# Up projections of a two-block network: the weight sums of rounds 1 to 21 made on GpSimd instead of VectorE

## The chip, the cores and the metric

The kernel runs on one core of a Trainium2 chip, as one program with five instruction streams: TensorE (PE in the profile; its weight loads are PEld), VectorE (DVE), ScalarE (ACT), GpSimd (POOL) and SyncE (SP), which issues the large weight transfers. The engines meet only through semaphores. The metric is the device time of one execution in microseconds (us), the median of several runs; lower is better. All data is fp32.

## The reference, cut to what matters

The program computes two blocks after each other on a sequence of 512 tokens with 1024 features. The first has two layers, each a mixer and a gated feed-forward network with a causal convolution of three taps:

```
def _conv_ffn(h, w_up, conv_w, conv_b, w_down):        # h: 512 x 1024, D_FF = 2816
    u, v = jnp.split(h @ w_up, 2, axis=-1)
    uc = conv_b + sum(shifted(u, j) * conv_w[j] for j in range(3))
    return (jax.nn.silu(uc) * v) @ w_down

for l in range(2):
    mod = silu(c) @ ada_w[l] + ada_b[l]                # six modulation vectors
    ...
    h = x * (1.0 + sc2) + sh2
    y = _conv_ffn(h, ffn_w_up[l], ffn_conv_w[l], ffn_conv_b[l], ffn_w_down[l])
    x = _layer_norm(ALPHA * x + g2 * y, ln_g[l, 1], ln_b[l, 1])
```

The second block (a recurrent and Fourier mixer, then a retention layer) follows and is not touched. What matters here is `h @ w_up`, twice, and the product `c @ ada_w`, which is spread over other stages in small tiles.

## The kernel before, in words

**The up projection.** `w_up` of a layer comes in 22 slabs of 1 MB, each with 128 columns of u and 128 of v. One slab is one round (`n` from 0 to 21). TensorE computes a round by Strassen's scheme in Winograd's form: the slab is a 2 by 2 grid of blocks (u or v, even or odd row blocks), the activations H another (even or odd row blocks, first or second half of the tokens). Seven block products take the place of eight; each is 4 matmuls of 128x128 weights by 256 columns, and each matmul stands in the profile as two instructions, so a round is 56 of them. The price is sums of blocks. Four "left sums" are needed for each slab, four tensor_tensor operations of 128x512 elements (lines 660 to 663). Round `n` writes them to buffer `LS[n % 2]`. The "right sums" of H are made once a layer.

**The order on TensorE** (`ffn_pe`). Each round from 1 on: wait for the slab; two products that need no left sums (16 instructions); wait for "left sums" `n`; two products with sums; two more; a last one. At its end the slab's slot is free. There are two slots, so SyncE issues slab `n + 2` when round `n` ends.

**The order on VectorE** (`ffn_dve`). In each round it first makes the left sums of round `n + 1`, then adds the products out of PSUM (lines 770 to 779: 256 columns each, one operand in SBUF and one in PSUM), applies two taps (781, 782), works on modulation tiles (350, or 354 and 357), and multiplies by the gate (788). The taps, the modulation work and line 788 have two operands in SBUF. ScalarE copies the first product, applies one tap and the SiLU.

**Modulation tiles.** `ada_w` comes as tiles of 128x1024 (512 KB), issued by GpSimd (line 377) into three buffers `late[j % 3]`. The issue of tile `j` waits for VectorE to be done with tile `j - 3`. VectorE uses two tiles a round in layer 0 (one operation each), one tile a round in layer 1 (two operations).

**GpSimd** (`ffn_pool`). In the up projection of a layer it issues tiles up to those for round 10, makes the four right sums of the first down projection (`first_right_pool`, 128x1024 elements each, from the results of rounds 0 to 7), issues tiles up to those for round 19, and then makes, for each of 12 steps of the down projection, that step's left sums, with tiles issued between them.

The two buffers of the left sums lie elsewhere: `LS[1]` takes the place of R, which ScalarE reads until it has written the last block of XA (line 629). So the sums of round 1 wait for the event ("norm", l, 0) "x" 7.

Of the kernel before, what the change touches and what calls it, by code (L numbers as in the profile page):

```python
# [9 lines left out]
ALU = mybir.AluOpType  # L10
# [5 lines left out]
DT = D // P  # L16
# [5 lines left out]
FT = FF // P  # L22
# [124 lines left out]
PE, DVE, ACTE, POOL = "pe_done", "dve_done", "act_done", "pool_done"  # L147
# [7 lines left out]
class Core:  # L155
# [53 lines left out]
    def p(self, name, a=0, n=None):  # L209
        at, size = P_AT[name]  # L210
        return self.par[:, at + a:at + a + (size - a if n is None else n)]
# [39 lines left out]
def settled(k, ins, *event):  # L251

    ins.then_inc(*k.says(DVE, *event))
    k.nc.vector.wait_ge(*k.now(DVE))
# [59 lines left out]
def dense_dve(k, name, n_tiles, splits, evac, first=0, deep=None):  # L314
# [3 lines left out]
    for n in range(n_tiles):  # L318
# [6 lines left out]
ADA_UP = [[range(N_ADA[0] + 2 * n, N_ADA[0] + 2 * n + 2) for n in range(FT)],  # L325
          [range(N_ADA[0] + 61 + n, N_ADA[0] + 62 + n) for n in range(FT)]]
# [15 lines left out]
def ada_tile_dve(k, j):  # L342

    v = k.nc.vector
    v.wait_ge(*k.when("ada in", j))
    part, tile = ada_home(j)
    w = k.early[:, j % EARLY, :] if j < N_EARLY else k.late[:, j % LATE, :]
    bias = k.p(("ada_b0", "ada_b1", "ada_b2_0", "ada_b2_1")[part], tile, 1)
    if part < 2:
        v.tensor_tensor_reduce(w, w, k.c_row[:], 1.0, bias, ALU.mult, ALU.add, k.MOD[part][:, tile, :])\  # L350
            .then_inc(*k.says(DVE, "ada used", j))
    else:
        v.wait_ge(*k.when("ada used", j - 1))
        v.tensor_tensor_reduce(k.junk[:], w, k.c2_rows[:, 0, :], 1.0, bias, ALU.mult, ALU.add, k.MOD2[part - 2][:, tile, 0:1])\
            .then_inc(*k.says(DVE))
        v.wait_ge(*k.now(DVE))
        v.tensor_tensor_reduce(w, w, k.c2_rows[:, 1, :], 1.0, bias, ALU.mult, ALU.add, k.MOD2[part - 2][:, tile, 1:2])\  # L357
            .then_inc(*k.says(DVE, "ada used", j))
# [12 lines left out]
def late_tiles_pool(k, first, last):  # L371

    g = k.nc.gpsimd
    for j in range(first, last):
        if j >= N_EARLY + LATE:
            g.wait_ge(*k.when("ada used", j - LATE))
        g.dma_start(k.late[:, j % LATE, :], k.dram["ada_rest"][j]).then_inc(*k.lands(f"late_in{j % LATE}", "ada in", j))  # L377


def ffn_pool(k, l, first):  # L380

    def issued(until):
        nonlocal first
        last = min(until + LATE, N_ADA[0] + 96)
        late_tiles_pool(k, first, max(first, last))
        first = max(first, last)
    issued(ADA_UP[l][10].stop)
    first_right_pool(k, l)
    issued(ADA_UP[l][FT - 3].stop)
    for it in range(ND):  # L390
        down_left_pool(k, l, it)
        issued(ADA_UP[l][FT - 1].stop if it == 0 else ADA_DOWN[l][it - 1].stop)
    issued(ADA_DOWN[l][-1].stop)
# [239 lines left out]
def left_blocks(k, l, n):  # L633

    wv = k.slab_view(f"w_up{l}", n, DT, 2 * P).rearrange("p (i e) (m n) -> p i e m n", e=2, m=2)
    return {(m, e): wv[:, :, e, m, :] for m in range(2) for e in range(2)}


def right_block(k, e, s, i0=0, i1=4):
    return k.H[:, 2 * i0 + e:2 * i1:2, s * HALF:(s + 1) * HALF]  # L640
# [6 lines left out]
def product(k, n, j):  # L647
    bank, s = PRODUCT_AT[j]
    return k.ps[:, 4 * (n % 2) + bank, s * HALF:(s + 1) * HALF]


def left_sums_dve(k, l, n):

    v, A, S = k.nc.vector, left_blocks(k, l, n), k.LS[n % 2]
    v.wait_ge(*k.when("slab", k.slab(f"w_up{l}", n)))
    if n >= 2:
        v.wait_ge(*k.when("products", l, n - 2, 3))
    elif n == 1:
        v.wait_ge(*k.when(("norm", l, 0), "x", DT - 1))
    v.tensor_tensor(S[:, 2, :, :], A[0, 0], A[1, 0], ALU.subtract).then_inc(*k.says(DVE))  # L660
    settled(k, v.tensor_tensor(S[:, 0, :, :], A[1, 0], A[1, 1], ALU.add))
    settled(k, v.tensor_tensor(S[:, 1, :, :], S[:, 0, :, :], A[0, 0], ALU.subtract))
    v.tensor_tensor(S[:, 3, :, :], A[0, 1], S[:, 1, :, :], ALU.subtract).then_inc(*k.says(DVE, "left sums", l, n))  # L663


def right_sums_dve(k, l, h):

    v, R = k.nc.vector, k.RS4
    v.wait_ge(*k.when(("norm", l, 0), "h", 4 * h + 3))
    B = {(e, s): right_block(k, e, s, 2 * h, 2 * h + 2) for e in range(2) for s in range(2)}  # L670
    t1, t2, t3, t4 = (R[:, j, 2 * h:2 * h + 2, :] for j in range(4))
    v.tensor_tensor(t3, B[1, 1], B[0, 1], ALU.subtract).then_inc(*k.says(DVE))
    settled(k, v.tensor_tensor(t1, B[0, 1], B[0, 0], ALU.subtract))
    settled(k, v.tensor_tensor(t2, B[1, 1], t1, ALU.subtract))
    v.tensor_tensor(t4, B[1, 0], t2, ALU.subtract).then_inc(*k.says(DVE, "right sums", l, h))
# [80 lines left out]
def ffn_dve(k, l):  # L756

    v = k.nc.vector
    v.memset(k.U[:, :, 0:2], 0.0).then_inc(*k.says(DVE, "ffn pad", l))
    for h in range(2):  # L760
        right_sums_dve(k, l, h)
    for n in range(FT):
        U, C, X, V = k.U[:, n % 2, :], k.C[:, n % 2, :], k.PX, k.PV
        p = lambda j: product(k, n, j)
        w = lambda j: k.p(f"conv{l}", 4 * n + j, 1)
        if n + 1 < FT:
            left_sums_dve(k, l, n + 1)
        first = k.P1[:, n % 2, :]
        v.wait_ge(*k.when("first product", l, n))
        v.tensor_tensor(U[:, 2:HALF + 2], first, p(2), ALU.add).then_inc(*k.says(DVE))  # L770
        v.wait_ge(*k.when("products", l, n, 1))
        settled(k, v.tensor_tensor(X[:, 0, :], first, p(6), ALU.add))
        settled(k, v.tensor_tensor(X[:, 1, :], X[:, 0, :], p(5), ALU.add))
        v.wait_ge(*k.when("products", l, n, 2))
        v.tensor_tensor(U[:, HALF + 2:T + 2], X[:, 1, :], p(3), ALU.add).then_inc(*k.says(DVE, "ffn u", l, n))  # L775
        settled(k, v.tensor_tensor(X[:, 2, :], X[:, 0, :], p(7), ALU.add))
        v.wait_ge(*k.when("products", l, n, 3))
        v.tensor_tensor(V[:, 0:HALF], X[:, 2, :], p(4), ALU.add).then_inc(*k.says(DVE))
        v.tensor_tensor(V[:, HALF:T], X[:, 2, :], p(5), ALU.add).then_inc(*k.says(DVE, "ffn v", l, n))
        v.wait_ge(*k.when("ffn tap", l, n))  # L780
        settled(k, v.scalar_tensor_tensor(C, U[:, 1:T + 1], w(1), C, ALU.mult, ALU.add))
        v.scalar_tensor_tensor(C, U[:, 0:T], w(0), C, ALU.mult, ALU.add).then_inc(*k.says(DVE, "ffn conv", l, n))
        if l == 0 and n == 0:
            v.wait_ge(*k.when("c2"))
        for j in ADA_UP[l][n]:
            ada_tile_dve(k, j)
        v.wait_ge(*k.when("ffn silu", l, n))
        v.tensor_tensor(k.G[:, n, :], C, V[:], ALU.mult).then_inc(*k.says(DVE, "ffn g", l, n))
# [27 lines left out]
def down_left_pool(k, l, it):  # L816

    g, (h, q) = k.nc.gpsimd, DOWN[it]
    A, S = down_left(k, l, it)
    g.wait_ge(*k.when("slab", k.slab(f"w_down{l}_{h}", q)))  # L820
    if it:
        g.wait_ge(*(k.when("down products", l, it - 2, 3) if it >= 2 else k.when("products", l, FT - 1, 3)))
    g.tensor_tensor(S[1], A[1, 0], A[1, 1], ALU.add).then_inc(*k.says(POOL))
    g.wait_ge(*k.now(POOL))
    g.tensor_tensor(S[2], S[1], A[0, 0], ALU.subtract).then_inc(*k.says(POOL))
    g.tensor_tensor(S[3], A[0, 0], A[1, 0], ALU.subtract).then_inc(*k.says(POOL))
    g.wait_ge(*k.now(POOL))
    g.tensor_tensor(S[4], A[0, 1], S[2], ALU.subtract).then_inc(*k.says(POOL, "down left", l, it))


def first_right_pool(k, l):

    g = k.nc.gpsimd
    B, R = down_right(k, 0)
    g.wait_ge(*k.when("ffn g", l, 7))
    g.tensor_tensor(R[1], B[0, 1], B[0, 0], ALU.subtract).then_inc(*k.says(POOL))
    g.wait_ge(*k.now(POOL))
    g.tensor_tensor(R[2], B[1, 1], R[1], ALU.subtract).then_inc(*k.says(POOL))
    g.tensor_tensor(R[3], B[1, 1], B[0, 1], ALU.subtract).then_inc(*k.says(POOL))
    g.wait_ge(*k.now(POOL))  # L840
    g.tensor_tensor(R[4], B[1, 0], R[2], ALU.subtract).then_inc(*k.says(POOL, "down right", l, 0))
# [3173 lines left out]
```

## Time and profile before

| | us |
|---|---|
| median of 3 runs (2493.9 to 2502.34) | 2498.15 |
| profiled execution, device time | 2495.48 |
| span of that execution's trace | 2494.1 |
| busy in the span: PE / DVE / ACT / POOL | 2334.1 / 1659.2 / 640.2 / 235.9 |

The span runs from the first to the last instruction; some 1.4 us of the device time lie around it. The up projection of layer 0 runs from about 360 to 631 us of the span, that of layer 1 from about 828 to 1100 us. The chain of work that ended last is TensorE for 84% and VectorE for 11%; the up projections' matmuls (line 683) alone are 20% of it. A wait of another engine costs time only if TensorE comes to wait in its turn.

In the rows below, "left_sums<-ring" means: writes the tile left_sums, reads the slab's slot. A bracket at the end of a line is the time that the engine sat idle before it, and what ended that.

### The profile page before, as it was taken

To read this page: it belongs to the slowest core of one execution; us is meant where nothing else is said; L and a number is where in the kernel's file an instruction comes from. 1 tells how busy PE (TensorE), PEld (TensorE's weight loads), DVE (VectorE), ACT (ScalarE), POOL (GpSimd) and SP (SyncE) were. 2 spreads that over 40 slices of the span, in tenths; PEclk is the share of its full clock that TensorE was granted. 3 is DMA by queue.
4 is the path that set the end of the run, shared out by engine and by line. 5 is a ranking of instruction groups with operands and counts; after the bars stand their busy time and mean duration, and the time that the engine had idled before them with its cause. 6 is when DMAs were issued, how large, how long until landed. Compare 5 with 4: busy or idle time off the path is not lost.

```text
span 2494.1 us, 39647 instructions
## 1 busy us (share of the span) xinstructions
PE 2334.1 (94%) x17066; PEld 1693.8 (68%) x17066; DVE 1659.2 (67%) x2800; ACT 640.2 (26%) x1314; POOL 235.9 (9%) x261
## 2 busy tenths in 40 slices
PE   7988889999997999999999999999997999999997
PEld 3675548888884688888756676676675654546973
DVE  3784378798799888879847879779787123232442
ACT  1323331111002311111043354444444212101111
POOL 2000000020541002024400000000000000000000
PEclk9999999999999999999999999999998999999999
DMA  8232135555432233343221101001010212111102
GB/s 329 90 113 76 60 134 169 172 170 181 161 131 89 85 128 126 135 139 132 95 98 70 40 19 35 21 20 37 3 36 19 85 51 84 51 52 66 35 18 101
DMA packets 42224, 227.99 MB, mean 91 GB/s; under 512 B 4737, under 2 KB 4865, under 8 KB 25793
## 3 DMA queue, kind: packets, MB, share of 16 engines
q1 hardware_dynamic: 21456, 140.56, 15.7%
q0 software_dynamic: 20016, 82.79, 9.8%
q8 instruction: 135, 2.21, 0.4%
q10 hardware_dynamic: 576, 2.11, 0.3%
q14 instruction: 41, 0.33, 0.0%
HBM read 219.14 MB, written 6.29 MB: 90 GB/s over the span
## 4 chain that ended last, share of the span: by engine, by line
PE 84%; DVE 11%; ACT 2%; issue 2%; DMA 1%; POOL 0%; SPq 0%; DVEq 0%; ACTq 0%; POOLq 0%
PE ps L683 20%; PE ps L2283 10%; PE ps L905 8%; PE ps L307 7%; PE ps L3383 3%; PE ps L2064 3%; PE ps L1039 3%; PE ps L455 2%; PE ps L1715 2%; PE ps L3572 2%; PE ps L2293 2%; PE ps L2302 2%; PE ps L3003 1%; PE ps L2971 1%; PE ps L2990 1%
## 5 line engine op out<-in xcount | busy, mean ns | idle before, releaser
L2283 PE MATMUL ps<-H,ring 128*128 128x256 f32 (+1 forms) x832 | 271.4, 487 | 5.4 <-ACT LW L2502 2.6
L683 PE MATMUL ps<-right_sums,left_sums 128*128 128x256 f32 x1056 | 242.8, 379 | 2.7 <-DVE left_sums L663 2.7
L2283 PEld LDWEIGHTS ps<-H,ring 128*128 128x128 f32 x832 | 157.4, 190 | 112.9 <-issue 92.8
L683 PEld LDWEIGHTS ps<-right_sums,left_sums 128*128 128x128 f32 x1056 | 200.5, 190 | 30.6 <-DVE left_sums L663 3.5
L307 PE MATMUL ps<-H,ring 128*128 128x512 f32 (+1 forms) x480 | 181.5, 535 | 0.9 <-DVE ls_tmp L3250 0.9
L683 PE MATMUL ps<-H,ring 128*128 128x256 f32 x704 | 164.2, 385 | 12.7 <-ACT H L626 12.7
L905 PE MATMUL ps<-G,ring 128*128 128x256 f32 x704 | 159.8, 379 | 0.0
L683 PEld LDWEIGHTS ps<-H,ring 128*128 128x128 f32 x704 | 134.6, 192 | 35.6 <-issue 12.8
L307 PEld LDWEIGHTS ps<-H,ring 128*128 128x128 f32 x480 | 91.1, 190 | 88.3 <-issue 84.9
L905 PEld LDWEIGHTS ps<-G,ring 128*128 128x128 f32 x704 | 133.8, 190 | 18.2
L377 POOL DMA_DIRECT2D ada_late<-ada_rest x104 | 56.2, 540 | 684.7 <-DVE mod L357 373.5
L750 ACT ACTIVATE C<-U,params_sb 128x512 f32<-128x512 f32 x44 | 35.9, 816 | 314.9 <-DVE U L775 314.9
L683 PE MATMUL ps<-H,left_sums 128*128 128x256 f32 x352 | 86.9, 388 | 0.0
L3383 PE MATMUL ps<-ring,H 128*128 128x256 f32 x384 | 85.9, 379 | 0.0
L2064 PE MATMUL ps<-O,ring 128*128 128x512 f32 (+1 forms) x256 | 83.6, 486 | 0.6 <-DVE H L2007 0.6
L683 PE MATMUL ps<-right_sums,ring 128*128 128x256 f32 x352 | 83.5, 379 | 0.0
L2007 DVE TENSOR_SCALAR H<-ps,scalars 128x512 f32<-128x512 f32 (+1 forms) x24 | 15.3, 661 | 97.7 <-ACT sq_ctx L2024 61.2
L3383 PEld LDWEIGHTS ps<-ring,H 128*128 128x128 f32 x384 | 72.0, 190 | 12.1 <-issue 3.1
L683 PEld LDWEIGHTS ps<-H,left_sums 128*128 128x128 f32 x352 | 68.2, 194 | 10.8 <-ACT H L626 1.4
L350 DVE CUSTOM_DVE_ANT_0 ada_late<-ada_late,c_row,params_sb 128x1024 f32<-128x1024 f32 x56 | 69.9, 1280 | 6.3 <-DMA ada_late<-ada_rest 6.2
L683 PEld LDWEIGHTS ps<-right_sums,ring 128*128 128x128 f32 x352 | 66.9, 190 | 9.1
L2064 PEld LDWEIGHTS ps<-O,ring 128*128 128x128 f32 x256 | 48.5, 190 | 34.0 <-issue 30.6
(593 smaller groups left out, 4704.2 us busy)
## 6 DMA issues: line engine op xcount, KB each, us to landing
ada_late<-ada_rest POOLq DMA_DIRECT2D x104, 512.0 KB, 3.7
ring<-w_up SPq DMA_DIRECT2D x44, 1024.0 KB, 4.8
ring<-w_down SPq DMA_DIRECT2D x16, 1024.0 KB, 4.9
ring<-od_in SPq DMA_DIRECT2D x16, 1024.0 KB, 4.8
ring<-ev_in SPq DMA_DIRECT2D x15, 1024.0 KB, 4.8
ada_early<-ada_rest POOLq DMA_DIRECT2D x24, 512.0 KB, 4.7
ada_first_sb<-ada_first SPq DMA_DIRECT2D x8, 1024.0 KB, 16.3
ring<-ab_in SPq DMA_DIRECT2D x7, 1024.0 KB, 6.4
```

The lines of the kernel that those rows point to most:

```text
L307: mm = pe.matmul(k.ps[:, (n % deep) * nb + b, 0:tn], wv[:, kk, a * P:(a + 1) * P], rhs[:, kk, t0:t0 + tn], start=(kk == 0), stop=(kk == kt ...
L350: v.tensor_tensor_reduce(w, w, k.c_row[:], 1.0, bias, ALU.mult, ALU.add, k.MOD[part][:, tile, :])\
L377: g.dma_start(k.late[:, j % LATE, :], k.dram["ada_rest"][j]).then_inc(*k.lands(f"late_in{j % LATE}", "ada in", j))
L455: mm = pe.matmul(k.ps[:, n, :], k.W8[:, kk, n * P:(n + 1) * P], k.H[:, kk, 0:T], start=(kk == 0), stop=(kk == DT - 1))
L683: return pe.matmul(product(k, n, j), lhsT[:, i, :], rhs[:, i, :], start=(i == 0), stop=(i == 3))
L905: mm = pe.matmul(product(k, it, j), left[:, i, :], right[:, i, :], start=(i == 0), stop=(i == ni - 1))
L1039: mm = pe.matmul(k.ps[:, bank, :], wv[:, kk, (i % 2) * P:(i % 2 + 1) * P], k.H[:, kk, 0:T], start=(kk == 0), stop=(kk == DT - 1))
L1715: return pe.matmul(out, wv[:, kk, (n % 2) * P:(n % 2 + 1) * P], rhs, start=start, stop=stop)
L2064: mm = k.nc.tensor.matmul(k.ps[:, 2 * (n % 2) + b, 0:tn], wv[:, kk, (n % 2) * P:(n % 2 + 1) * P], k.O[:, kk, t0:t0 + tn], start=(start and ...
L2283: mm = pe.matmul(k.ps[:, bank + b, 0:tn], wv[:, kk, (i % 2) * P:(i % 2 + 1) * P], k.H[:, kk, t0:t0 + tn], start=(kk == 0), stop=(kk == DT ...
L2293: mm = k.nc.tensor.matmul(k.ps[:, bank + n, 0:tn], lhsT, rhs[:, t0:t0 + tn], start=True, stop=True)
L3383: mm = pe.matmul(k.ps[:, 3 + 4 * (u % 2), 0:256], k.H[:, kk, t * P:(t + 1) * P], wv[:, kk, :], start=(kk == 0), stop=(kk == DT - 1))
```

## The change

The left sums of round 0 stay on VectorE (they are made before the stage). Those of rounds 1 to 21 move to GpSimd, with the same four operations in another order, and the tiles' issue is put between them: after the sums of round `n`, the tiles up to those for round `n - 2`, plus three. `first_right_pool` comes after the sums of round 12 and the issue behind them.

```
 def ffn_pool(k, l, first):
...
-    issued(ADA_UP[l][10].stop)
-    first_right_pool(k, l)
+    issued(ADA_UP[l][0].start)
+    for n in range(1, FT):
+        left_sums_pool(k, l, n)
+        if n >= 2:
+            issued(ADA_UP[l][n - 2].stop)
+        if n == 12:
+            first_right_pool(k, l)
     issued(ADA_UP[l][FT - 3].stop)
...
+def left_sums_pool(k, l, n):
+
+    g, A, S = k.nc.gpsimd, left_blocks(k, l, n), k.LS[n % 2]
+    g.wait_ge(*k.when("slab", k.slab(f"w_up{l}", n)))
+    g.wait_ge(*(k.when("products", l, n - 2, 3) if n >= 2 else k.when(("norm", l, 0), "x", DT - 1)))
+    g.tensor_tensor(S[:, 0, :, :], A[1, 0], A[1, 1], ALU.add).then_inc(*k.says(POOL))
+    g.wait_ge(*k.now(POOL))
+    g.tensor_tensor(S[:, 1, :, :], S[:, 0, :, :], A[0, 0], ALU.subtract).then_inc(*k.says(POOL))
+    g.tensor_tensor(S[:, 2, :, :], A[0, 0], A[1, 0], ALU.subtract).then_inc(*k.says(POOL))
+    g.wait_ge(*k.now(POOL))
+    g.tensor_tensor(S[:, 3, :, :], A[0, 1], S[:, 1, :, :], ALU.subtract).then_inc(*k.says(POOL, "left sums", l, n))
...
 def ffn_dve(k, l):
...
-        if n + 1 < FT:
-            left_sums_dve(k, l, n + 1)
         first = k.P1[:, n % 2, :]
```

## Rows read from the trace of the kernel before

**Rows 1.** Busy time per engine and instructions (x) of one stretch: PE, PEld, DVE, ACT, POOL, clock, DMA
```profile
870.00:970.00 100.00, 100.00 (x465) 88.04 (x464) 80.89 (x150) 15.57 (x26) 4.26 (x9) 1.00 0.40 136
```

**Rows 2.** Waits of TensorE over the span: who waited for whom, us, times, longest
```profile
PE ps L902 <- DVE H L984: 5.2, 2, 2.7
...
PE ps L905 <- DVE down_right_last L861: 3.8, 2, 2.7
PE ps L905 <- POOL ring L828: 3.1, 3, 1.4
...
PE ps L683 <- DVE left_sums L663: 2.7, 2, 1.4
```

**Rows 3.** TensorE in order of time, around round 12 of each layer: start, length
```profile
508.89 3.62 PE L683 MATMUL ps<-H,ring 128*128 128x256 f32 x16
513.78 1.56 PE L683 MATMUL ps<-right_sums,left_sums 128*128 128x256 f32 x6 [1.27 <-DVE left_sums L663]
...
964.68 3.62 PE L683 MATMUL ps<-H,ring 128*128 128x256 f32 x16
...
976.77 3.62 PE L683 MATMUL ps<-H,ring 128*128 128x256 f32 x16
981.78 3.72 PE L683 MATMUL ps<-right_sums,left_sums 128*128 128x256 f32 x16 [1.40 <-DVE left_sums L663]
```

**Rows 4.** VectorE in the same time, layer 1
```profile
965.62 0.74 DVE L781 SCALAR_TENSOR_TENSOR C<-U,params_sb,C 128x512 f32<-128x512 f32 x1
...
967.07 1.28 DVE L354 CUSTOM_DVE_ANT_0 junk<-ada_late,c_rows,params_sb 128x1024 f32<-128x1024 f32 x1
...
969.60 0.69 DVE L788 TENSOR_TENSOR G<-C,product_v 128x512 f32<-128x512 f32 x1
970.21 3.25 DVE L660 TENSOR_TENSOR left_sums<-ring 128x512 f32<-128x512 f32 x1
```

**Rows 5.** GpSimd in the same time: the four right sums of the first down projection
```profile
970.53 2.37 POOL L836 TENSOR_TENSOR down_right<-G 128x1024 f32<-128x1024 f32 x1
972.97 2.70 POOL L838 TENSOR_TENSOR down_right<-G,down_right 128x1024 f32<-128x1024 f32 x1
...
978.50 2.67 POOL L841 TENSOR_TENSOR down_right<-G,down_right 128x1024 f32<-128x1024 f32 x1
```

**Rows 6.** One operation of the left sums, all 44: ns min/median/max
```profile
L660 DVE TENSOR_TENSOR left_sums<-ring x44: 682/686/3245, 351.4 to 1080.7; 128x512 f32<-128x512 f32 x44
```

**Rows 7.** GpSimd: tile issues, and first and last of four sums of a down step
```profile
629.69 1.10 POOL L377 DMA_DIRECT2D ada_late<-ada_rest  x2
...
1093.03 1.26 POOL L823 TENSOR_TENSOR down_left<-ring 128x512 f32<-128x512 f32 x1 [12.07 <-DMA ring<-w_down]
...
1096.94 1.27 POOL L828 TENSOR_TENSOR ring<-ring,down_left 128x512 f32<-128x512 f32 x1
```

**Rows 8.** SyncE's slab issues from 964 on, and the time to landing of w_up slabs
```profile
964.88 26.16 SPq L273 DMA_DIRECT2D ring<-w_up  x3
...
DMA to landing us min/median/max: 4.6/4.8/6.0
```

**Rows 9.** DMA issues from 340 to 620 us: modulation tiles, median us to landing
```profile
ada_late<-ada_rest POOLq DMA_DIRECT2D x41, 512.0 KB, 4.2
```

**Rows 10.** GpSimd and VectorE late in the down steps, in order of time
```profile
701.54 0.99 POOL L826 TENSOR_TENSOR ring<-ring 128x384 f32<-128x384 f32 x1
...
1216.77 1.98 POOL L826 TENSOR_TENSOR ring<-ring 128x384 f32<-128x384 f32 x1
...
1215.99 1.90 DVE L354 CUSTOM_DVE_ANT_0 junk<-ada_late,c_rows,params_sb 128x1024 f32<-128x1024 f32 x1
```

**Rows 11.** VectorE and TensorE at round 1 of layer 1, in order of time
```profile
839.53 0.69 DVE L660 TENSOR_TENSOR left_sums<-ring 128x512 f32<-128x512 f32 x1 [1.58 <-ACT XA L629]
...
843.82 3.62 PE L683 MATMUL ps<-H,ring 128*128 128x256 f32 x16
847.27 3.62 PE L683 MATMUL ps<-right_sums,left_sums 128*128 128x256 f32 x16
```

## The prediction

> **What bounds the kernel now.** I read the views in this order: busy time by stretch, TensorE's waits, then the engines in order of time around the places where TensorE waits. The first shows a TensorE that is busy for all of a 100 us stretch of up projection at full granted clock, while VectorE is busy for 80.9 us of it and GpSimd for 4.3 [rows 1]. A round starts every 12.09 us (964.68 to 976.77 [rows 3]). So the 80.9 us are not a bound as such: shortening VectorE's work gains only where TensorE waits for it. Of such waits on the left sums there are two in the whole trace, 2.7 us together [rows 2], one in each layer, in round 12. In other rounds the products with sums start 3.45 us after the round does (843.82 to 847.27 [rows 11]). In round 12 it is 4.89 us in layer 0 and 5.01 us in layer 1 [rows 3], so 1.44 and 1.56 us late, 3.0 us in all. The cause stands beside it: GpSimd makes its four right sums from 970.53 to 981.17, and VectorE's left sums, 0.69 us by their median [rows 6], take 3.25 us there [rows 4, 5]. Everything else that the change touches is hidden behind TensorE.
>
> **What is removed.** 42 sets of left sums with four operations each leave VectorE: 168 x 0.69 us = 116 us, or 2.8 us of each round. All but the two sets at round 12 lie beside TensorE's work, so 113 us of them are worth nothing. What is worth something is the 3.0 us above, and only if nothing else is late at that place.
>
> **What is added in an ordinary round.** I count from the start of TensorE's round n - 1. SyncE issues slab n at +0.2 us, and it lands 4.8 us later, at +5.0 [rows 3, 8]. GpSimd has no left sums of w_up in the trace, but it does the same four operations on the same 128x512 shapes in the down steps: from 1093.03 to 1098.21, 5.2 us [rows 7]. The lower bound is that. VectorE's line 788, with two operands in SBUF, starts about +4.9 (969.60 in the round of 964.68 [rows 3, 4]), so I add 0.4 us for one collision: done at +10.6. The sums are wanted at 12.09 + 3.45 = +15.5. That leaves 4.9 us of cover. Two things could eat it. The tiles are now issued behind the sums, at +10.6 and +11.2 (0.55 us each [rows 7]) in place of right behind VectorE's use, and each takes 4.2 us to land [rows 9]: they are in flight when SyncE issues the next slab at +12.3. Bounds for what that adds to the slab: nothing, or at most a whole tile's 4.2 us, and the sums are then done at +14.8, still in time. And the collisions with VectorE could be four rather than one: next to VectorE's operations of 1.90 us a GpSimd operation takes 1.98 us where the same one takes 0.99 us elsewhere [rows 10], so 1.0 us each and 5.2 + 4.0 = 9.2 us, done at +14.2. Only both together miss. I take 0 us of TensorE's time for each of the 40 ordinary rounds.
>
> What waits behind the sums in GpSimd's queue is the tile issue. In layer 0 a tile issued at +11.2 lands at +15.4, or +3.3 of the next round, where VectorE, relieved of its sums, wants its second tile at about +3.7: no wait, or one of 1 us that ends long before round n + 2 wants the products read out. In layer 1 the tiles are a round ahead. The issue itself waits for a tile used in the round before, long done.
>
> **Round 1.** The sums wait for ScalarE's last XA block and started on VectorE at 839.53. On GpSimd they end at 839.5 + 5.2 = 844.7, and are wanted at 847.27 [rows 7, 11]: 2.6 us of cover in layer 1. Layer 0 has the same pattern with slightly less. Cost 0, at most 1 us.
>
> **Round 13, where it gets tight.** The four right sums (10.64 us, 970.53 to 981.17 [rows 5]) now stand between the left sums of rounds 12 and 13 in one in-order queue. Counted from the start of round 11: sums of round 12 done at +10.6; tiles issued until +11.7 in layer 0 (two) and +11.2 in layer 1 (one); right sums until +22.3 and +21.8; left sums of round 13 until +27.5 and +27.0. They are wanted at 2 x 12.09 + 3.45 = +27.6. So without more collisions this just fits. But VectorE now comes with its taps, its modulation operations and line 788 (0.74, 1.28 and 0.69 us [rows 4]; two taps, two modulation operations, one product) in the middle of GpSimd's chain. The 10.64 us hold some collision already: three operations took 2.67 to 2.80 us where the first took 2.37 [rows 5]. By rows 10 a modulation operation costs GpSimd 0.9 to 1.0 us; two of them 1.8 and line 788 0.4, less 0.7 for the two smaller collisions they replace, gives 1.5 us. Done at +29.0 and +28.5: TensorE waits 1.4 and 0.9 us, 2.3 in all. Bounds: nothing, and all eight operations hit by 1.0 us each, less the 1.0 us in the 10.64: 7.0 us more, +34.5 and +34.0, so waits of 6.9 and 6.4 us, 13.3 in all. I lean to the lower end, since VectorE has five such operations a round and they cannot meet eight. VectorE loses some 6 us there, but the products of round 12 need only be read out before round 14. Rounds 14 on start with GpSimd back in step, 4 us ahead of the need.
>
> **What the Trainium skill says.** The trace has a VectorE operation of 0.69 us stretched to 3.25 us beside one of GpSimd of 2.4 us [rows 4 to 6]. The Trainium skill (SBUF — State Buffer, "Who interferes with whom") makes that a lock on a shared read interface: an operation with two SBUF inputs on VectorE and a reading one on GpSimd exclude each other for whole instructions. The trace agrees that they exclude each other; that GpSimd pays the other's full length it does not show (1.0 us beside 1.90 us [rows 10]). The rule has a rival of its own below.
> The rows make GpSimd 5.2 us for sums that cost VectorE 2.8 us [rows 6, 7]. The Trainium skill (GPSIMD Engine Reference, "Engine selection") speaks against the change: elementwise work with two inputs belongs on VectorE, GpSimd being about twice as slow. The trace agrees on the ratio (1.9); the price matters only in the chain of round 13.
>
> **The sum.** The profiled execution took 2495.48 us (span 2494.1 and 1.4 around it). Gone: 3.0 us. New: 2.3 us. That gives 2494.8 us, 0.7 less. The median of the runs shown is 2.7 us above the profiled one, and they spread over 8.4 us; against the median the forecast is 2497.4 us.
>
> **Rivals.**
> - Forecast: the wait moves from VectorE's sums in round 12 to GpSimd's in round 13. Change -3 to +3 us. Chance 0.67.
> - The chain of round 13 fits: no new wait, 3.0 us gained, 2495.1 us. For it: uncollided it ends 0.1 and 0.6 us early. Against it: VectorE's operations are due in its middle. Chance 0.08.
> - Full exclusion: each of VectorE's five operations in the chain of round 13 holds GpSimd up for its own length, 2 x 0.74 + 2 x 1.28 + 0.69 = 4.7 us [rows 4], in place of 1.5. The chain ends at +32.2 and +31.7, waits 4.6 and 4.1 us, so 8.7 - 3.0 = +5.7 us: 2503.9 us. For it: VectorE's 0.69 us became 2.7 to 3.25 us beside GpSimd. Against it: the 1.0 us of rows 10, and the order in which the two happen to start. Chance 0.10. (This is what the lock of the Trainium skill, SBUF — State Buffer, "Who interferes with whom", would give.)
> - The other side: GpSimd's queue at round 13 slips by its upper bound, each of its eight operations held up by VectorE, which is itself held up and so never out of the way. 13.3 - 3.0 = +10.3 us, 2508.5 us. It decides from a slip of 5.6 us a layer on (waits of 3.0 + 7.5 = 10.5 us, and the 0.7 us by which the chains are early, over two layers). For it: late in the down steps whole runs of operations alternate at 1.9 us [rows 10]. Against it: the supply of VectorE operations. Chance 0.06. With it I put the case in which ordinary rounds fail too: slab late by 4.2 us and four collisions, done at +18.4, 2.9 us late in each of 40 rounds, 116 us, less the 3.0: 2611 us. Against it: the down steps run these sums at TensorE's pace with 3.1 us of waits [rows 2]. Chance 0.04.
> - VectorE's head start carries into the down steps, where TensorE waits 5.2 + 3.8 + 3.1 = 12.1 us [rows 2]: 2497.4 - 12.1 = 2485.3 us. Against it: there VectorE waits for products anyway, so what it is ahead is lost at the first of them. Chance 0.05.
>
> **Chances and range.** A measurement of this kernel tells a change from none at about 0.3%, 7.5 us. The forecast, the second case and full exclusion lie within it (0.67 + 0.08 + 0.10 = 0.85, a point of it given to the spread of the runs: 0.84); faster 0.06; slower 0.10. The range: 3.0 us of gain and the spread of the runs below, 2490; the 10.3 us above, 2508.
>
> **What would show it.** In the trace after: no 3.25 us operation in VectorE's left sums, none after round 0 at all; GpSimd with 168 more operations of about 1.3 us, busy some 220 us more; sums starting 5 us into each round; one TensorE wait on GpSimd's left sums in each layer, at round 13, of 1 to 2 us; rounds at 12.09 us else. The prediction is wrong if TensorE waits for left sums in ordinary rounds, if slabs land later than 9 us after their issue, or if round 13's wait passes 5 us.

## The result and the profile after

The changed kernel takes 2503.28 us (median of 20 runs, 2498.87 to 2506.61), the kernel before 2498.43 us (20 runs, 2493.9 to 2502.34). The ratio is 1.0018, 95% interval 1.0011 to 1.0025: slower by 4.5 us, 2.7 to 6.2 us (the medians lie 4.85 us apart). The forecast was 0.7 us faster. It lies outside the interval, on the other side of zero, although the change is smaller than the 0.3% that the text called the same.

The totals say that the change did what it says: 168 instructions more on GpSimd and as many fewer on VectorE. First section of the profile of the changed kernel (busy us, share of the span, instructions):

```profile
span 2504.5 us, 39646 instructions
PE 2339.9 (93%) x17066; PEld 1697.5 (68%) x17066; DVE 1584.9 (63%) x2632; ACT 639.1 (26%) x1314; POOL 472.0 (19%) x429
```

VectorE is busy 74 us less, not 116: its other operations became longer beside GpSimd (the 44 products by the gate took 30.3 us together before, 47.1 us now). Of TensorE's waits, those that answer to [rows 2] in the changed kernel (us in total, times, longest):

```profile
PE ps L701 <- POOL left_sums L681: 5.9, 2, 3.1
PE ps L918 <- DVE H L1000: 5.2, 2, 2.7
...
PE ps L921 <- DVE down_right_last L877: 4.0, 2, 2.6
PE ps L921 <- POOL ring L844: 3.1, 3, 1.4
```

The two waits on VectorE's left sums are gone, two on GpSimd's have come, and the waits of the down steps have not moved. TensorE around round 13 of the changed kernel, layer 0 and then layer 1, in order of time (start, length):

```profile
521.11 3.62 PE L701 MATMUL ps<-H,ring 128*128 128x256 f32 x16
527.51 5.41 PE L701 MATMUL ps<-right_sums,left_sums 128*128 128x256 f32 x16 [2.78 <-POOL left_sums L681]
532.75 1.89 PE L701 MATMUL ps<-H,left_sums 128*128 128x256 f32 x8
...
992.47 3.62 PE L701 MATMUL ps<-H,ring 128*128 128x256 f32 x16
999.20 5.34 PE L701 MATMUL ps<-right_sums,left_sums 128*128 128x256 f32 x16 [3.12 <-POOL left_sums L681]
1004.38 1.89 PE L701 MATMUL ps<-H,left_sums 128*128 128x256 f32 x8
```

Two losses are to be read here. The products with sums start 6.40 and 6.73 us into the round in place of 3.45: 2.95 and 3.28 us late. And the 16 instructions then take 5.24 us (527.51 to 532.75) and 5.18 us in place of 3.45: 1.79 and 1.73 us more. Granted clock in stretches of the changed kernel (the first number behind the last bracket, in front of the DMA share; first the wait, then the slow stretch, then what follows; then the slow stretch of layer 1):

```profile
524.60:527.50 2.90, 0.13 (x1) 0.00 (x0) 2.83 (x6) 0.81 (x1) 2.82 (x4) 1.00 0.26 107
527.50:532.70 5.20, 5.19 (x16) 4.30 (x17) 5.16 (x5) 0.89 (x2) 5.11 (x5) 0.67 0.59 202
532.70:540.00 7.30, 7.30 (x35) 6.42 (x35) 7.16 (x12) 0.82 (x1) 4.16 (x4) 1.00 0.39 120
...
999.20:1004.30 5.10, 5.10 (x16) 4.26 (x17) 5.03 (x5) 0.89 (x2) 5.00 (x4) 0.68 0.33 104
```

TensorE had stood idle for 2.8 us, and then ran 5.2 us at a mean of 0.67: partly at the upper level of 2.4 GHz, partly at the lower of 1.2. The kernel before showed nothing of this after its waits of 1.27 and 1.40 us [rows 3]; its 16 instructions took 3.72 us by their row, the next ones came after 3.56, so 0.11 us were lost.

The sum for the up projections: 4.74 and 5.01 us lost in round 13, against 1.55 and 1.67 us in round 12 before (1.44 + 0.11, 1.56 + 0.11), so 6.5 us more in the profiled execution. The chain of work confirms it: layer 0's up projection from its first unbroken stretch to its end took 264.69 us before and 267.89 us after. The whole difference of the two spans, 10.4 us, holds 3.9 us more that lie outside the up projections, most of them in the second block, which the change does not touch; single executions of one kernel differ by 8 us. I take the ratio of all runs for the total and the trace for the place. The two do not quite meet: the 6.5 us that the trace places lie just above the interval's end of 6.2. Whether the other executions were spared part of it, a slow stretch for instance, no run shows.

**Why the chain was late.** GpSimd from the landing of slab 12 on, layer 1 of the changed kernel:

```profile
975.79 1.26 POOL L676 TENSOR_TENSOR left_sums<-ring 128x512 f32<-128x512 f32 x1 [8.42 <-DMA ring<-w_up]
977.13 1.26 POOL L678 TENSOR_TENSOR left_sums<-left_sums,ring 128x512 f32<-128x512 f32 x1
978.35 1.27 POOL L679 TENSOR_TENSOR left_sums<-ring 128x512 f32<-128x512 f32 x1
979.70 1.27 POOL L681 TENSOR_TENSOR left_sums<-ring,left_sums 128x512 f32<-128x512 f32 x1
980.92 0.57 POOL L377 DMA_DIRECT2D ada_late<-ada_rest  x1
981.51 2.36 POOL L852 TENSOR_TENSOR down_right<-G 128x1024 f32<-128x1024 f32 x1
983.95 2.70 POOL L854 TENSOR_TENSOR down_right<-G,down_right 128x1024 f32<-128x1024 f32 x1
986.61 2.80 POOL L855 TENSOR_TENSOR G<-G 128x1024 f32<-128x1024 f32 x1
989.49 3.21 POOL L857 TENSOR_TENSOR down_right<-G,down_right 128x1024 f32<-128x1024 f32 x1
992.66 2.25 POOL L676 TENSOR_TENSOR left_sums<-ring 128x512 f32<-128x512 f32 x1
994.99 1.60 POOL L678 TENSOR_TENSOR left_sums<-left_sums,ring 128x512 f32<-128x512 f32 x1
996.55 1.26 POOL L679 TENSOR_TENSOR left_sums<-ring 128x512 f32<-128x512 f32 x1
997.89 1.26 POOL L681 TENSOR_TENSOR left_sums<-ring,left_sums 128x512 f32<-128x512 f32 x1
```

The first group is undisturbed: 1.26 us each, 5.1 us in all. From 981.51 on GpSimd never rests, and where its operations are longer (2.70 and 2.80 in place of 2.36, then 3.21, 2.25, 1.60), VectorE is at work on two SBUF operands. VectorE in the same time:

```profile
981.32 3.10 DVE L797 SCALAR_TENSOR_TENSOR C<-U,params_sb,C 128x512 f32<-128x512 f32 x1
984.46 2.73 DVE L798 SCALAR_TENSOR_TENSOR C<-U,params_sb,C 128x512 f32<-128x512 f32 x1
987.12 3.38 DVE L354 CUSTOM_DVE_ANT_0 junk<-ada_late,c_rows,params_sb 128x1024 f32<-128x1024 f32 x1
...
990.53 3.25 DVE L357 CUSTOM_DVE_ANT_0 ada_late<-ada_late,c_rows,params_sb 128x1024 f32<-128x1024 f32 x1
...
993.71 1.74 DVE L804 TENSOR_TENSOR G<-C,product_v 128x512 f32<-128x512 f32 x1
```

One operation of each engine pairs with one of the other: 0.75 us become 3.10 and 2.73, 1.28 us become 3.38 and 3.25. The two modulation operations are what lengthens GpSimd's 3.21 and 2.25 us. Five operations of VectorE lengthen five of GpSimd, by 0.34, 0.44, 0.85, 0.98 and 0.33 us: each by what was left of VectorE's operation when GpSimd's started, less 0.13 to 0.16 us (the second modulation operation ends at 993.78, 1.12 us after the left sum starts at 992.66; that sum takes 0.98 us more).

### The profile page after: what moved, and what is told of

Read it like the earlier page. It is cut to its first block, busy times and chain, and to the rows that moved or that the text cites. A ratio compares the mean times of both kernels' runs of the same rounds, so it can differ in the third digit from the quotient of the medians.

```text
span 2504.5 us, 39646 instructions
## 1 busy us (share of the span) xinstructions
PE 2339.9 (93%) x17066; PEld 1697.5 (68%) x17066; DVE 1584.9 (63%) x2632; ACT 639.1 (26%) x1314; POOL 472.0 (19%) x429
## 4 chain that ended last, share of the span: by engine, by line
PE 83%; DVE 10%; POOL 2%; issue 2%; ACT 2%; DMA 1%; SPq 0%; DVEq 0%; ACTq 0%; POOLq 0%
PE ps L701 19%; PE ps L2299 10%; PE ps L307 7%; PE ps L921 7%; PE ps L3399 3%; PE ps L2080 3%; PE ps L1055 3%; PE ps L460 2%; PE ps L1731 2%; PE ps L3588 2%; PE ps L2309 2%; PE ps L2318 2%; PE ps L3019 1%; PE ps L2987 1%; PE ps L3006 1%
## 5 line engine op out<-in xcount | busy, mean ns | idle before, releaser
L676 POOL TENSOR_TENSOR left_sums<-ring 128x512 f32<-128x512 f32 x42 | 57.8, 1377 | 293.5 <-DMA ring<-w_up 191.2
L350 DVE CUSTOM_DVE_ANT_0 ada_late<-ada_late,c_row,params_sb 128x1024 f32<-128x1024 f32 x56 | 80.7, 1454 | 37.6 <-DMA ada_late<-ada_rest 37.5
```

The lines of the kernel that those rows point to most:

```text
L676: g.tensor_tensor(S[:, 0, :, :], A[1, 0], A[1, 1], ALU.add).then_inc(*k.says(POOL))
```

## The experiments

After the first reading I held this theory: all the loss sits in one in-order chain on GpSimd (left sums of round 12, tile issue, four right sums, left sums of round 13), and the terms of that chain add up. The rivals were a cost in every round (late slabs, late tiles), and a worth of VectorE's freed time. Four of the kernels below ran once each (2499.94, 2492.49, 2506.30 and 2506.64 us, in their order); of those only the traces are read, not the totals.

**The right sums spread over four rounds.** In the changed kernel:

```
-        if n == 12:
-            first_right_pool(k, l)
+        if 10 <= n < 14:
+            first_right_part(k, l, n - 10)     # one of its four operations
```

> The changed kernel, with the four right sums of the first down projection issued one each behind the left sums of rounds 10, 11, 12 and 13 instead of all four behind round 12. Theory (queue): all of the loss is the one in-order chain of round 13, which made TensorE wait 2.78 and 3.12 us and then run 5.2 us at a granted clock of 0.67. One operation of 2.4 to 3.2 us fits into the gap in which GpSimd waits for the next slab, so both waits and both slow stretches go: 6.5 us less than the changed kernel in the two up projections, and since the waits of round 12 in the kernel before are gone too, 3.2 us less than before: ratio to before 0.9987, about 2495 us. Rival (ordinary rounds): late slabs and late modulation tiles cost in every round; the ratio stays at 1.001 or above though TensorE waits for no left sums. Rival (second block): the difference comes from elsewhere in the span, the ratio stays 1.0018.

Measured: ratio 0.9987 (0.9977 to 0.9997), 2495.38 us. TensorE waits for no left sums at all. The chain of work of this kernel (start, us, what) runs through the 22 rounds of layer 0 in one piece:

```profile
365.98 263.15 PE ps L701 x1218
```

Against the 264.69 us before and the 267.89 us of the changed kernel these are 1.54 and 4.74 us less, the two sums of losses above. This kernel makes its left sums on GpSimd in 42 rounds, and no round of layer 0 costs anything. In layer 1 its rounds run in one piece too, 266.50 us from 829.90 on. The rival of a cost in every round is out.

**The same spread in the kernel before**, left sums still on VectorE:

```
-    issued(ADA_UP[l][10].stop)
-    first_right_pool(k, l)
+    for i in range(4):
+        issued(ADA_UP[l][9 + i].stop)
+        first_right_part(k, l, i)
```

> The kernel before, with left sums still on VectorE, and only the four right sums spread: one each behind the tile issue of rounds 9, 10, 11 and 12 on GpSimd. This takes away the collision of round 12 without moving any left sum. Theory (queue): each of VectorE's operations is held up at most once a round by 2 to 3 us, which its slack hides; the waits of 1.27 and 1.40 us go: 3.2 us less than before, ratio 0.9987, and the same as the changed kernel with the same spread, so that moving the left sums is worth nothing by itself. Rival (freed VectorE): moving the sums has a worth of its own, and this kernel is slower than the spread one with sums on GpSimd by more than 0.1%. Rival (ordinary rounds): it is faster than that one by 3 us or more.

Measured: ratio 0.9987 (0.9978 to 0.9996), 2492.67 us. The same ratio as with the sums on GpSimd; the medians lie 2.7 us apart, in favour of the sums on VectorE, which is less than the runs of one kernel differ by. So no worth of moving the 168 operations, alone, shows within about 0.13%, and the 3 us that can be had come from spreading the four right sums, without it.

**The right sums on VectorE**, one at the end of each of its rounds 9 to 12 (in the changed kernel; `first_right_pool` is gone):

```
         v.tensor_tensor(k.G[:, n, :], C, V[:], ALU.mult).then_inc(*k.says(DVE, "ffn g", l, n))
+        if 9 <= n < 13:
+            first_right_dve(k, l, n - 9)
```

> The changed kernel, with the four right sums of the first down projection made by VectorE, one each at the end of its rounds 9 to 12, where it now has time. GpSimd's queue then holds left sums and tile issues alone. Theory (queue): no wait on left sums in any round, no slow stretch, 3.2 us less than before, ratio 0.9987, the same as the spread kernel. GpSimd's left sums take 5.1 to 7.5 us in every round, wanted 15.5 us after the slab's issue. Rival (ordinary rounds): ratio 1.001 or above.

Measured: ratio 0.9987 (0.9978 to 0.9995), 2494.34 us; no wait for left sums. Three ways to take the right sums out of the chain give the same time.

**Short modulation operations in rounds 11 and 12** (32 of 1024 columns in `tensor_tensor_reduce`, for those tiles only; the two operations of a tile in layer 1 are cut in the same way):

```
+    N = SHORT if any(j in ADA_UP[l][n] for l in range(2) for n in (11, 12)) else D
-        v.tensor_tensor_reduce(w, w, k.c_row[:], 1.0, ...)
+        v.tensor_tensor_reduce(w[:, 0:N], w[:, 0:N], k.c_row[:, 0:N], 1.0, ...)
```

> The changed kernel, but VectorE's modulation operations of rounds 11 and 12 work on 32 of the 1024 columns (those modulation values are then not the reference's): 1.28 us each become some 0.2 us. GpSimd's queue is unchanged. Theory (collisions): the chain of round 13 ended 2.9 to 3.3 us late because VectorE's operations with two SBUF operands held up GpSimd's: the last right sum took 3.22 us in place of 2.7, the first left sum 2.25 in place of 1.27, the second 1.60. With short ones the last right sum takes about 2.7, the two left sums 1.3 each, and the chain ends 1.5 to 1.8 us earlier: TensorE waits 1.2 to 1.6 us instead of 2.8 and 3.1, and no slow clock follows. Rival (length of the queue alone): the chain ends where it did, the waits stay at 2.8 and 3.1 us.

Measured, in one execution: waits of 1.65 and 2.45 us. TensorE of this kernel, both layers:

```profile
525.44 3.72 PE L703 MATMUL ps<-right_sums,left_sums 128*128 128x256 f32 x16 [1.65 <-POOL left_sums L683]
...
996.92 5.41 PE L703 MATMUL ps<-right_sums,left_sums 128*128 128x256 f32 x16 [2.45 <-POOL left_sums L683]
```

From the first right sum to the last left sum the chain took 16.2 us in both layers (509.11 to 525.34, 980.62 to 996.80), where the changed kernel had 17.6 us in both. So the modulation operations cost it 1.4 us; I had expected 1.5 to 1.8. Collisions are one term. In layer 0 the slow stretch is gone. In layer 1 it is not, and both the wait and the clock that I had expected are missed: slab 12 landed late there, the left sums of round 12 began 8.2 us into round 11. That is a second term.

**The tile issue ahead of the left sums.** With the issue behind them, a tile starts 1 to 2 us ahead of the next slab in about every second round. Time from issue to landing of the w_up slabs in layer 0, changed kernel, against a median of 4.8 us in [rows 8]:

```profile
DMA to landing us min/median/max: 4.7/5.7/8.5
```

The edit:

```
-        left_sums_pool(k, l, n)
         if n >= 2:
+            k.nc.gpsimd.wait_ge(*k.when("slab", k.slab(f"w_up{l}", n)))
             issued(ADA_UP[l][n - 2].stop)
+        left_sums_pool(k, l, n)
```

> The changed kernel, but the tiles of a round are issued when the round's slab has landed, ahead of its left sums, in place of behind them; the right sums stay behind round 12. Theory (three parts of the slip): the tiles issued 1 to 2 us ahead of a slab made it land after 7 to 8.5 us in about every other round; round 12 of layer 1 was such a one (7.3 us), round 12 of layer 0 was not. With the issue right after landing, slabs land in 4.7 to 5.6 us in all rounds. The chain to round 13 is then the same in both layers, some 2.5 us shorter in layer 1: a wait of 1 to 2 us there in place of 3.12, about the same as before (2.8) or up to 1 us less in layer 0, and a slow stretch only where the wait is above some 2 us. Ratio to before 0.9995 to 1.0010. Rival (landing does not matter): both waits stay near 3 us and the ratio at 1.0018.

Measured: ratio 1.003 (1.002 to 1.0039), waits of 2.81 and 3.34 us. Both the expected ratio and the expected wait of layer 1 are missed, though the slabs do land earlier (median 4.7 and 4.8 us). GpSimd shows what I had overlooked, between the last right sum and the left sums of round 13 in layer 1:

```profile
986.63 3.22 POOL L858 TENSOR_TENSOR down_right<-G,down_right 128x1024 f32<-128x1024 f32 x1
991.49 0.57 POOL L377 DMA_DIRECT2D ada_late<-ada_rest  x1 [1.65 <-PE ps L702]
992.09 1.29 POOL L677 TENSOR_TENSOR left_sums<-ring 128x512 f32<-128x512 f32 x1
```

The issue waits until VectorE is done with an earlier tile, and VectorE was held up until 990.86 by those very right sums. The profile puts the wait down to TensorE; by the program it is the event "ada used", and the modulation operation had ended 0.6 us before. So 1.65 us of idling and 0.57 us of issue stood in the chain against the 1.6 us by which it started earlier and 0.5 us that the left sums met less of VectorE's work. The run did not test its question.

**The same, with round 13's issue behind its sums again:**

```
-        if n >= 2:
+        if n >= 2 and n != 13:
...
         left_sums_pool(k, l, n)
+        if n == 13:
+            issued(ADA_UP[l][n - 2].stop)
```

> As the kernel with the tile issue ahead of the left sums, but in round 13 the issue stands behind the sums again. In that earlier kernel GpSimd stood still for 1.65 us between the right sums and the left sums of round 13 (the issue waits for VectorE's modulation work, which the right sums held up) and issued for 0.57 us, which used up the 1.6 us that the earlier landing of slab 12 had given in layer 1, so it did not tell. Theory (landing is one term of the chain): without that wait the chain of layer 1 is 5.9 (landing) + 0.6 + 5.2 + 11.2 + 5.2 to 6.4 = 28.1 to 29.3 us against 27.6, a wait of 0.5 to 1.7 us in place of 3.12, and TensorE stays at full granted clock there. Layer 0 the same within 1 us, unless its two issues (1.1 us) come on top. Ratio to before 0.9990 to 1.0005. Rival (landing does not matter): a wait near 3 us and the slow stretch in layer 1, ratio 1.0018 or more.

Measured: ratio 1.0001 (0.9992 to 1.001). TensorE of this kernel in both layers, then the slabs' landing in layer 0:

```profile
525.33 3.72 PE L704 MATMUL ps<-right_sums,left_sums 128*128 128x256 f32 x16 [1.43 <-POOL left_sums L684]
...
994.61 3.72 PE L704 MATMUL ps<-right_sums,left_sums 128*128 128x256 f32 x16 [1.55 <-POOL left_sums L684]
```

```profile
DMA to landing us min/median/max: 4.6/4.8/4.8
```

Chain from the first right sum to the last left sum: 17.6 us again in both layers. It only begins earlier, 11.7 us into round 11 in layer 1 (976.94 - 965.27) in place of 13.2 us. In layer 1 that is the landing of slab 12, 5.9 us into the round in place of 7.5; in layer 0 it is the left sums of round 12, which took 5.2 us in place of 6.6. The waits are near those of the kernel before, the slow stretches are gone, and the time is that of the kernel before. The place of the tile issues alone takes the ratio from 1.0018 to 1.0001.

**No tile issue in the chain** (round 12's goes with round 13's):

```
-        if n >= 2:
+        if n >= 2 and n != 12:
```

> The changed kernel without the tile issue between the left sums of round 12 and the right sums (those tiles are issued one round later). It takes 1.1 us (two issues, layer 0) and 0.57 us (one, layer 1) out of the chain of round 13. Theory (queue): the waits fall from 2.78 to 1.7 us and from 3.12 to 2.5 us, less or more by what the shifted chain meets of VectorE's operations (1 us). The slow stretch after the wait, which followed waits of 2.45, 2.78 and 3.12 us and not those of 1.27, 1.40 and 1.65, stays away in layer 0. Rival (the chain is not what ends the wait): no change.

Measured, in one execution: waits of 0.15 and 1.59 us, and no slow stretch; 1.7 and 2.5 us had been expected. They fell by 2.63 and 1.53 us, more than the 1.1 and 0.57 us taken out. In layer 0 the rest is collisions: the left sums of round 13 took 1.26, 1.27, 1.26 and 1.27 us, since the chain, begun earlier, met fewer of VectorE's operations, and the stretch was 16.3 us. In layer 1 it was 17.6 us as ever, and the chain began 1.5 us earlier, of which the left-out issue is 0.57 us and the landing of slab 12 the rest. The chain ends the wait, as expected, but its terms do not stand still when one is taken out.

**One right sum made twice:**

```
-    g.tensor_tensor(R[3], B[1, 1], B[0, 1], ALU.subtract).then_inc(*k.says(POOL))
-    g.wait_ge(*k.now(POOL))
+    for _ in range(2):
+        g.tensor_tensor(R[3], B[1, 1], B[0, 1], ALU.subtract).then_inc(*k.says(POOL))
+        g.wait_ge(*k.now(POOL))
```

This sum is written over one of its own operands (G<-G in the profile), so the second making spoils its values; only times are read.

> The changed kernel with one of the four right sums made twice, 2.8 us more in the chain of round 13. Theory (queue): every us of it is waited for, so TensorE waits about 5.6 us in layer 0 and 5.9 us in layer 1. For the slow clock: if what follows a wait is a stretch of fixed length, the 16 instructions after it take 5.2 us again (1.8 us lost); if it grows with the wait, the loss is 3 us or more. Sum: 2 x 2.8 = 5.6 us more than the changed kernel, or up to 9 us more.

Measured, in one execution: waits of 5.35 and 5.37 us. TensorE of this kernel in layer 0:

```profile
528.14 5.92 PE L701 MATMUL ps<-right_sums,left_sums 128*128 128x256 f32 x16 [5.35 <-POOL left_sums L681]
533.89 1.89 PE L701 MATMUL ps<-H,left_sums 128*128 128x256 f32 x8
```

The start is 5.5 us late in both layers, 2.6 and 2.3 us more than in the changed kernel. The chain is 2.75 us longer in both layers (20.3 in place of 17.6 us) and began 0.2 and 0.5 us earlier in its round, so all of the added time is waited for. The 16 instructions take 5.75 us (528.14 to 533.89): 2.3 us lost to the clock. Neither reading that I had laid out is right: the loss is not fixed at 1.8 us, and it did not grow to the 3 us or more that I had set for the other.

**The right sums behind round 17:**

```
-        if n == 12:
+        if n == 17:
```

> The changed kernel with the four right sums behind the left sums of round 17 in place of 12. Theory (queue): the same wait of 1.5 to 3.5 us, now in round 18, in each layer, followed by a slow stretch if it is above 2 us; none in round 13; the same time as the changed kernel within 2 us. It depends on which phase of the landing pattern round 17 meets. Rival (something peculiar to round 12, such as the modulation tiles used there): no wait.

Measured, in one execution: waits in round 18, of 3.99 and 1.55 us, the first followed by a slow stretch, the second not; none in round 13. The first lies above the 1.5 to 3.5 us expected. The place moves with the right sums, so nothing about round 12 is special. The sum, 5.5 us, is near the 5.9 us of the changed kernel; why it divides so was not looked into.

## Why the prediction was wrong

Its place was right: no wait in ordinary rounds, none in round 1, one wait in each layer, in round 13, on GpSimd's left sums; the 3.0 us of before gone; and the down steps untouched. What failed is the size of one term, "TensorE waits 1.4 and 0.9 us, 2.3 in all", and a term that the sum did not have, the clock after such a wait. The waiting measured 2.95 and 3.28 us of late start, 6.2 in all, mostly because the late landing of slab 12 in layer 1 and the left sums' own collision in layer 0 had been put at next to nothing; and the clock took another 3.5 us. 2.3 became 9.75 us, and -0.7 us became +6.5 us in this execution (+4.5 by the ratio of all runs).

| step of the chain, us | predicted | layer 0 | layer 1 |
|---|---|---|---|
| slab 12 landed, sums begin | +5.0 | +5.1 | +7.5 |
| left sums of round 12 | 5.6 | 6.6 | 5.1 |
| tile issue | 1.1 / 0.55 | 1.1 | 0.6 |
| right sums | 10.6 and a share of 1.5 | 11.15 | 11.15 |
| left sums of round 13 | 5.2 and the rest of it | 6.4 | 6.4 |
| chain ends | +29.0 / +28.5 | +30.5 | +30.8 |

(Counted from the start of round 11, at 496.94 and 968.30 us.)

- **Landing.** I had bounded what the tiles do to the next slab at up to 4.2 us, found that ordinary rounds stand it, and took nothing. For round 13 the same term was taken at nothing again, where there was no cover. It was 2.5 us in layer 1. A bound carried for the case with 4.9 us of slack must be carried into the case with none. The kernel with the mixed issue order shows its worth in layer 1: 3.12 us of wait became 1.55.
- **Collisions in the chain.** 1.5 us were forecast, 1.75 measured in the right sums and the left sums of round 13 (17.55 us against 10.6 + 5.2); the short modulation operations show 1.4 us of it. This part was right. Not in the sum was the left sums' own collision in round 12 of layer 0, 6.6 us in place of 5.6: VectorE had waited 2.7 us for its second tile there, so that it was still at work. I had called such a wait harmless, and for TensorE in that round it was.
- **The clock.** The sum had no term for it. 1.79 and 1.73 us are a third of the whole loss of round 13. [rows 3] held waits of up to 1.40 us only, without effect, and I did not ask what a longer one does. The same trace held two, in the down steps of layer 1, one without and one with a slow stretch. TensorE of the kernel before, then the granted clock of the work behind each wait:

```profile
1177.87 2.83 PE L905 MATMUL ps<-down_right,down_left 128*128 128x256 f32 x12 [2.73 <-DVE down_right_last L861]
...
1241.63 3.47 PE L902 MATMUL ps<-H,consts_sb 128*128 128x512 f32 x4 [2.70 <-DVE H L984]
```

```profile
1177.87:1180.54 2.67, 2.67 (x13) 2.36 (x14) 2.49 (x5) 0.00 (x0) 0.00 (x0) 1.00 0.00 0
...
1241.60:1244.90 3.30, 3.27 (x4) 1.51 (x5) 2.05 (x3) 0.63 (x1) 0.00 (x0) 0.54 0.00 0
```

So the rivals with waits above 2.5 us needed a clock term of up to 1.8 us for each wait, and none had one. Had the waits been 1.4 and 0.9 us, the traces here give no reason for such a term, and the change would have come out near nothing, as in the kernel with the mixed issue order: waits of 1.43 and 1.55 us, ratio 1.0001.
- **The rivals.** The one nearest to the measured time is full exclusion, +5.7 us, and that is in part luck: it had neither the late slab nor the slow clock. Its mechanism was nearer than its chance of 0.10: all five of VectorE's operations did lengthen one of GpSimd's, by 2.94 us together where it had 4.7. But its sum added the 4.7 us to right sums of 10.64 us that held 1.0 us of collision already, without taking that off; the chain grew by 1.75 us over 10.6 + 5.2. The upper slip and the carry into the down steps did not come. "The chain fits" came about in none of the kernels with all right sums behind one round; nearest was 0.15 us in one layer.

The Trainium skill (SBUF — State Buffer, "SBUF: two separate sides") has whichever of the two starts first hold the shared ports for its whole instruction, with the other blocked. For VectorE the trace agrees: 0.75 us became 3.10 and 2.73 beside GpSimd's 2.4 to 2.8. For GpSimd it agrees in length: a left sum grew by 0.98 us beside the last 1.12 us of a modulation operation. By the starts in the trace it does not agree on who goes first: VectorE's tap started at 981.32, GpSimd's first right sum at 981.51, and it was the tap that was held up while the sum took its undisturbed 2.36 us.

## What to carry to other kernels

In an in-order queue, find the longest piece of work that stands between two deadlines and sum the whole chain up to the second one, with every term at its upper bound, before looking at the averages: GpSimd was busy 19% of the time, and one chain of it set the result. Moving work off an engine that nobody waits for gained nothing here; what gained here was cutting a block of four operations into four single ones, each put into a gap (0.9987, with the sums on either engine). And a longer wait of TensorE can have a second price, a fall of the granted clock: two waits of 1.5 us and two of 3 us differed by 6.2 us of lost time in these traces, not by 3. Between 2.2 and 2.75 us that second price came in some kernels and not in others, so near there carry it as a bound and not as a sum.

## What the runs showed of the hardware

- **Waits of TensorE and the clock after them**, in the middle of an up projection, over all these kernels (one execution each). After 0.15, 1.27, 1.40, 1.43, 1.55 (twice), 1.59 and 1.65 us of idling the next 16 instructions took 3.56 us. After 2.45, 2.78, 2.81, 3.12, 3.34 and 3.99 us they took 5.08 to 5.25 us, after 5.35 and 5.37 us 5.75 and 5.77 us. The stretch behind the 3.99 us, in the kernel with the right sums behind round 17:

```profile
588.20:593.50 5.30, 5.26 (x17) 4.35 (x18) 5.18 (x4) 0.89 (x2) 5.21 (x5) 0.68 0.50 198
```

Up to the wait the engine had run without a gap at full granted clock, and it did nothing but wait before each of these stretches. The length of the wait alone does not decide. Where TensorE waits for down_right_last in the down projection of layer 1, waits of 2.24 to 2.73 us came before the same 12 instructions in all eleven traces. They took 2.66 or 2.67 us in five (waits of 2.24, 2.26, 2.37, 2.58 and 2.73 us) and 4.05 to 4.35 us in six (2.24, twice 2.25, 2.26, 2.59 and 2.72 us). What decides there was not found, so the slow stretches after 2.45 and 2.78 us may be chance too. The Trainium skill (TensorE: Matmul & The Clock Gate, "Part 1: The HAM clock gate (the "warmup" mystery)") has the array at full or at half rate by how busy it has been, nothing between; a mean of 0.67 to 0.68 over such a stretch fits a part at each level.
- **A tile and a slab in flight together.** A 1 MB transfer of SyncE behind a 512 KB transfer of GpSimd issued up to 2 us ahead landed after 7 to 8.5 us in place of 4.8. With the tiles issued at the slab's landing instead, the median of the slabs was 4.7 to 4.8 us again. In the changed kernel this fed back: a late slab made late sums and a late tile issue, which then missed the next slab, so that late and early landings took turns in most rounds (left sums began at 951.25, 961.60 and 975.79 us, 10.4 and 14.2 us apart, with rounds of 12.09 us).
- **GpSimd alone.** Its tensor_tensor of 128x512 takes 1.26 us and of 128x1024 2.36 us, VectorE's of 128x512 0.69 us: a ratio of 1.8, where the prediction worked with 5.2 over 2.8 us, 1.9.
- **VectorE and GpSimd together.** The program lets the engines meet only through semaphores, but in time these two also hold each other up, with no semaphore between them: the tap of 3.10 us and the left sum of 2.25 us above.
